# A joint input projection in exact fp32 passes, changed to split products with two block buffers

## The reference, cut to what matters

```
h_ctx = layernorm(ctx) * (1 + scale_c) + shift_c        # 256 context tokens, 1024 channels
h_x   = layernorm(x)   * (1 + scale)   + shift          # 256 tokens, 1024 channels
u     = concat(h_ctx, h_x)                              # 512 tokens
z, xbc, dt, rwkv, gq, gk, gv, gd, og = split(u @ w_in)  # w_in: 1024 x 3504, the joint projection
```

## Time and profile before

| what | value |
|---|---|
| median of three runs | 2103.74 us |
| the profiled execution, device time | 2110.86 us |
| its span, first to last instruction | 2109.1 us |
| mean granted TensorE clock | 0.939 of full speed |
| TensorE busy | 1927.0 us (91%) |
| joint projection, first to last matmul | 908.3 to 1143.3 us |

### The profile page before, as it was taken

How to read it: one execution, slowest core, us unless ns; L and a number is a source line. 1 busy time by engine, 2 the same in 40 slices (tenths; PEclk the granted TensorE clock), 3 DMA queues, 4 the chain that set the end, 5 groups by cost and what they waited for, 6 DMA issues and landing times.

```text
span 2109.1 us, 33698 instructions
## 1 busy us (share of the span) xinstructions
PE 1927.0 (91%) x14454; PEld 1399.7 (66%) x14454; DVE 1001.6 (47%) x1382; ACT 644.9 (31%) x1004; POOL 216.0 (10%) x218
## 2 busy tenths in 40 slices
PE   6878999899998899989999779989899999999992
PEld 5758999889997899855766658874344444444440
DVE  4664554555554677756545664663221121111116
ACT  4334333444443533330033531421111111111110
POOL 0000000000000000002100014401111111121213
PEclk9878999999997999999899679989999999999997
DMA  9313555544442777546511000066998998998886
GB/s 326 101 61 113 189 187 179 171 146 160 141 161 78 262 245 250 165 149 192 160 50 43 0 13 4 3 264 244 398 382 342 380 383 345 377 376 350 329 345 253
DMA packets 191893, 438.68 MB, mean 208 GB/s; under 512 B 24208, under 2 KB 145552, under 8 KB 162448
## 3 DMA queue, kind: packets, MB, share of 16 engines
q1 hardware_dynamic: 156336, 352.02, 45.4%
q0 software_dynamic: 23040, 43.05, 6.0%
q10 hardware_dynamic: 12384, 41.69, 5.1%
HBM read 501.68 MB, written 26.21 MB: 250 GB/s over the span
## 4 chain that ended last, share of the span: by engine, by line
PE 81%; DVE 9%; DMA 4%; ACT 3%; issue 2%; SPq 0%; POOL 0%; ACTq 0%; DVEq 0%; POOLq 0%
PE psum L344 30%; PE psum L3324 15%; PE psum L3345 7%; PE psum L1538 6%; PE psum L3295 4%; PE psum L1545 2%; DMA mem<-in_exp_w_dram 2%; PE psum L2555 2%; ACT w_hi L400 1%; DMA mem<-in_na_w_qkv_dram 1%; DVE mem L3445 1%; PE psum L2539 1%; DVE w_lo L405 1%; PE psum L3085 1%; PE psum L564 1%
## 5 line engine op out<-in xcount | busy, mean ns | idle before, releaser
L405 DVE TENSOR_TENSOR w_lo<-mem,w_hi 128x2048 fp32r<-128x2048 f32 x122 | 279.3, 2291 | 266.5 <-ACT w_hi L400 263.9
L344 PE MATMUL psum<-x_hi,w_hi 128*128 128x256 f32 x1216 | 353.5, 291 | 4.6 <-DVE x_lo L551 4.6
L3324 PE MATMUL psum<-mem 128*64 128x512 f32 x1536 | 341.4, 597 | 7.8 <-DMA mem<-in_exp_w_dram 7.8
L344 PE MATMUL psum<-x_hi,w_lo 128*128 128x256 f32 x1216 | 347.4, 286 | 0.0
L344 PE MATMUL psum<-x_lo,w_hi 128*128 128x256 f32 x1216 | 346.8, 285 | 0.0
L400 ACT ACTIVATE w_hi<-mem 128x2048 fp32r<-128x2048 f32 x122 | 233.8, 1918 | 202.4 <-PE psum L344 187.5
L3324 PEld LDWEIGHTS psum<-mem 128*64 128x64 f32 x1536 | 110.5, 138 | 230.8 <-issue 213.7
L344 PEld LDWEIGHTS psum<-x_hi,w_hi 128*128 128x128 f32 x1216 | 237.2, 195 | 11.3 <-DVE w_lo L405 4.9
L344 PEld LDWEIGHTS psum<-x_lo,w_hi 128*128 128x128 f32 x1216 | 240.9, 198 | 0.7
L344 PEld LDWEIGHTS psum<-x_hi,w_lo 128*128 128x128 f32 x1216 | 239.7, 197 | 0.0
L3345 PE MATMUL psum<-mem 128*64 128x512 f32 x768 | 175.4, 598 | 2.4 <-issue 1.8
(11 more groups left out here) (494 smaller groups left out, 2982.3 us busy)
## 6 DMA issues: line engine op xcount, KB each, us to landing
mem<-in_exp_w_dram SPq DMA_DIRECT2D x192, 1024.0 KB
mem<-in_dil_w_qkv_dram SPq DMA_DIRECT2D x36, 1024.0 KB, 5.3
mem<-in_ada_w_dram POOLq DMA_DIRECT2D x48, 512.0 KB, 4.7
y_rows<-mem ACTq DMA_DIRECT2D x48, 512.0 KB
mem<-in_ffn_w_gate_dram SPq DMA_DIRECT2D x22, 1024.0 KB, 5.7
mem<-in_ffn_w_up_dram SPq DMA_DIRECT2D x22, 1024.0 KB, 5.6
mem<-in_ffn_w_down_dram SPq DMA_DIRECT2D x22, 1024.0 KB, 4.8
mem<-in_w_in_dram SPq DMA_DIRECT2D x13, 1024.0 KB, 6.7
```

The source lines that it names most:

```text
L344: ins = pe.matmul(out, lhs[a], rhs[b], start=start and k == 0, stop=stop and k == 2, **kw)
L405: dve.tensor_tensor(w_lo[n % SLOTS][:, 0, :], ring[:, n % SLOTS, :], w_hi_f[n % HI][:, 0, :], ALU.subtract).then_inc(S("w_split"), 1)
L3324: ins = pe.matmul(psum[r, up, :].rearrange("p (a n) -> p a n", a=2), xg[:, b % 2, c, x * P + 64 * e:x * P + 64 * e + 64], w_up[s][e][:, :, ...
```

## The change

The projection is done in split products, and its buffers are arranged anew:

- The six ring slots get fixed roles. Slots 0 and 1 hold the raw and low parts of the activations (`u_raw`, `u_lo`), slots 2 and 3 the raw weight block of even and odd items (the low part is written over the raw one), slots 4 and 5 their high parts. So two blocks are in flight and not six: the load of block n (n of 2 or more) waits until block n-2 is used (`mix_in_sp`).
- Blocks 0 and 1 are cast and subtracted ahead of time (`mix_hi_act` in the first block's code on ScalarE, `mix_lo` on VectorE, block 1's behind the activations). For each later block the cast is put into ScalarE's list, and the subtraction into GpSimd's, at one half of a job of the block before: the first half of its second job, or the second half of its only job (`next_split`).
- The activations are split too: `ctx_hi_act`, `ctx_lo_dve`, `x_hi_act` (ScalarE, 8 chunks) and `x_lo_dve` (VectorE, two dependent operations for each of 8 chunks). TensorE's first job waits chunk by chunk.
- Block 0 is 128 columns wide in place of 32. The z blocks stand between xbc blocks and dt before the last xbc block. SyncE holds the loads of `w_out` until the projection is done.

```diff
-    mix_items = ([(GD0, 32, "chan"), (GQ0, 256, "chan"), (GV0, 256, "tok_all"), (OG0, 256, "tok_x")]
-                 + [(XBC0 + 256 * i, 256, "chan") for i in range(4)] + [(DT0, 16, "dt")]
-                 + [(Z0 + 256 * i, 256, "tok_x") for i in range(2)]
+    mix_items = ([(GD0, P, "chan"), (GQ0, 256, "chan"), (GV0, 256, "tok_all"), (OG0, 256, "tok_x"),
+                  (XBC0, 256, "chan"), (Z0, 256, "tok_x"), (XBC0 + 256, 256, "chan"), (Z0 + 256, 256, "tok_x"),
+                  (XBC0 + 512, 256, "chan"), (DT0, 16, "dt"), (XBC0 + 768, 256, "chan")]
                  + [(RW0 + 256 * i, 256, "chan") for i in range(4)] + [(RW0 + 1024, 128, "chan")])
...
     def mix_in_sp(sp):
-        for c0, w, _ in mix_items:
-            load(sp, cols(d["w_in_2"][0], c0, w), KC, w)
+        for m, (c0, w, _) in enumerate(mix_items):
+            n = MIX + m
+            sp.wait_ge(S("item_used"), n - SLOTS + 1 if m < 2 else n - 1)
+            sp.dma_start(slot(MIX_RAW[m % 2], KC, w), cols(d["w_in_2"][0], c0, w)).then_inc(S(f"slot_loaded{n % SLOTS}"), 16)
+            sp_items[0] += 1
+
+    def mix_hi_act(act, m):
+
+        n, w = MIX + m, KC * mix_items[m][1]
+        act.wait_ge(S(f"slot_loaded{n % SLOTS}"), 16 * (n // SLOTS + 1))
+        if m < 2:
+            act.wait_ge(S("item_used"), MIX - 3 + m)
+        act.activation(mix_hi[m % 2][:, 0, 0:w], ring[:, MIX_RAW[m % 2], 0:w], ACT.Copy).then_inc(S("w_hi"), 1)
+
+    def mix_lo(eng, m):
+
+        w = KC * mix_items[m][1]
+        eng.wait_ge(S("w_hi"), split_no(MIX + m))
+        eng.tensor_tensor(w_lo[MIX_RAW[m % 2]][:, 0, 0:w], ring[:, MIX_RAW[m % 2], 0:w], mix_hi_f[m % 2][:, 0, 0:w],
+                          ALU.subtract).then_inc(S("w_split"), 1)
...
+    def next_split(h):
+
+        m, part = divmod(h, 2)
+        n, k, parts = MIX_JOBS[m][:3]
+        return n + 1 if part == (0 if parts == 2 else 1) and k == parts - 1 and 2 <= n + 1 < len(mix_items) else None
...
-                ins = pe.matmul(psum[0:wd, b, 0:ALL], w[:, c, k * P:k * P + wd], uT[:, c, :], start=c == 0,
-                                stop=c == KC - 1)
+                if m == 0:
+                    if c == 0:
+                        pe.wait_ge(S("x_split"), X_NO["ctx"] + 2)
+                    x_part(pe, "x", c)
+                ins = split_product(pe, bank(b), [a[:, c, k * P:k * P + P] for a in w], [a[c // 4][:, c % 4, :] for a in u], c == 0,
+                                    c == KC - 1)
...
     def mixed_act(act):
-            if what == "move" and n % 2 == 0:
+            if what == "half" and next_split(n):
+                mix_hi_act(act, next_split(n))
+            elif what == "move" and n % 2 == 0:
...
     def mixed_pool(pool):
-            if what == "gla":
+            if what == "half" and next_split(n):
+                mix_lo(pool, next_split(n))
+            elif what == "gla":
...
     def block2_dve(dve):
         x_rows_dve(dve)
-        for c in range(1, KC, 2):
-            x_out(dve, c)
+        for h in range(2):
+            ctx_lo_dve(dve, h)
+        for c in range(KC):
+            x_lo_dve(dve, c)
+        mix_lo(dve, 1)
         mixed_dve(dve)
```

More of the change, by code:

```diff
@@ L132 @@
 SECOND_USE = {
+    "ctx_hi": ("na_bias_ready", 8),
     "sd_skip": ("sd_a", 1), "sd_xdt_n": ("sd_u", 1),
@@ L1288, in block1_act @@
         act.wait_ge(S("mod_in"), 16 * 8)
+        for m in range(2):
+            mix_hi_act(act, m)
         residual_act(act, MOD)
@@ L1319, in block1_dve @@
         mod_dve(dve)
+        mix_lo(dve, 0)
         residual_dve(dve)
@@ L1477, in program @@
     top[0] = stage_top
-    uT = alloc(KC, ALL)
+    u_hi_f, u_hi = zip(*(both(f"u_hi{h}", top[0] + 4 * h * ALL, 4, ALL) for h in range(2)))
+    u_lo = [both(f"u_lo{h}", ring_at + 4 * h * ALL, 4, ALL)[1] for h in range(2)]
+    u_raw = mem[:, ring_at:ring_at + KC * ALL].rearrange("p (c n) -> p c n", c=KC)
+    top[0] += KC * ALL
     ctx_tok = mem[:, mod_at + 6 * D:mod_at + 6 * D + NT * D].rearrange("p (t c) -> p t c", t=NT)
@@ L1511, in mix_jobs, with jobs_at @@
                         yield n, k, 2, xbcT[:, (c0 - XBC0) // P + k, :], 1.0
+    MIX_RAW, MIX_HI = (2, 3), (4, 5)
+    assert MIX % SLOTS == MIX_RAW[0] and W_OUT % SLOTS == 0
+    mix_hi_f, mix_hi = zip(*(both(f"mix_hi{q}", ring_at + q * SLOT, 1, SLOT) for q in MIX_HI))
     def mix_in_sp(sp):
-        for c0, w, _ in mix_items:
-            load(sp, cols(d["w_in_2"][0], c0, w), KC, w)
-    MIX_JOBS = list(mix_jobs())
-    J_OG, J_XBC, J_RW = 5, 6, 17
+        for m, (c0, w, _) in enumerate(mix_items):
[14 more added lines that the diff above has]
+                          ALU.subtract).then_inc(S("w_split"), 1)
+    MIX_JOBS = list(mix_jobs())
+    def jobs_at(lo, hi):
+        return [m for m, j in enumerate(MIX_JOBS) if lo <= mix_items[j[0]][0] < hi]
+    XBC_JOBS, RW_JOBS = jobs_at(XBC0, DT0), jobs_at(RW0, GQ0)
+    J_DT, J_RW, J_OG = jobs_at(DT0, RW0)[0], RW_JOBS[0], jobs_at(OG0, OG0 + 1)[0]
+    def next_split(h):
+        m, part = divmod(h, 2)
+        n, k, parts = MIX_JOBS[m][:3]
+        return n + 1 if part == (0 if parts == 2 else 1) and k == parts - 1 and 2 <= n + 1 < len(mix_items) else None
     def mix_moved(eng, m):
@@ L1544, in mix_half_pe @@
                 for c in range(KC):
-                    ins = pe.matmul(bank(b, width, a * width), uT[:, c, tiles[a] * P:(tiles[a] + 1) * P], w[:, c, :],
-                                    start=c == 0, stop=c == KC - 1)
+                    tok = slice(tiles[a] * P, (tiles[a] + 1) * P)
+                    ins = split_product(pe, bank(b, width, a * width), [v[c // 4][:, c % 4, tok] for v in u], [v[:, c, :] for v in w],
+                                        c == 0, c == KC - 1)
         if part == 1:
@@ L3475, in block2_act @@
         norm_n["act"] += 1
-        for c in range(0, KC, 2):
-            x_out(act, c)
+        for c in range(KC):
+            x_hi_act(act, c)
         mixed_act(act)
```

48 lines of the change are left out of this document (30 added, 18 removed).

## The result

The changed kernel takes 2145.35 us (median of 4 runs, 2135.7 to 2148.79) where the kernel before takes 2104.39 in the same comparison: 1.018 times as long by the ratio on record, 95% interval 1.015 to 1.021 (the two medians differ by 41 us, a factor of 1.019). The forecast was slower, 2130 us, 26 us above its own base; the direction is right, the size 15 us short. The profiled span is 2147.0 us, 37.9 longer than the one before.

A forecast was written before the change was run, and what follows sets the result against it. Projection bound by TensorE alone. Bookkeeping 255 against 233 us, +22, plus 1 for dt and 3 for the clock: +26, so 2137 us against the profiled 2110.86, 2130 us against the median; range 2104 to 2152 us.

The forecast's parts named there:

- TensorE's side: Projection matmuls: channel and token jobs save 28 and 6 us, dt costs 4 and 2 more; 28 us saved.
- When a block is ready: Blocks 1 to 15: cast and subtraction, 6.6 us with handovers, often come late; new kernel's stalls sum to 60 us.
- the hand sum: Block 12: ready at 1101.2, TensorE standing from 1091.3 after one 5.54 us job; a wait of 9.9 us.
- the bookkeeping: Projection: four queues carried forward entry by entry in list order; 255 us against 233 for the kernel before, +22.
- The waits that were there: Kernel before, projection: 6 us of stalls (1.4 + 5.0) taken off the new 60, leaving 54.
- The clock: Behind some five long stalls: up to 1.7 us each, 0 to 9 us together; 3 taken.
- Rival (c): Projection: clock stays low after stalls, 9 for 3, and late modulation rows add two per block for 8; 2152 us, chance 0.15.
- GpSimd against VectorE: Twelve full subtractions: each can hold a two-input VectorE operation for up to 4.52 us, the whole instruction.
- the sum with 41 us of stalls: Projection: VectorE gets through beside GpSimd's subtractions, as by a shared port; stalls 41 us, not 60.
- Rival (a): Projection: VectorE is not held by the long subtraction; 237 against 233 us in the bookkeeping, 2112 us, chance 0.17.
- Rival (b): Blocks 4 to 10: casts reached one half earlier, TensorE idle under 10 us; -18, 2086 us, chance 0.13.
- Nothing behind the projection: After the projection: nothing moves; `w_out` is loaded from 1143 on and used after 1331.

The follow-up runs named there:

- Experiments 6: Changed kernel with all subtractions on VectorE, block 12's split ahead of the modulation sum, and dt as a channel job: 2105.90 us, 1.0004 of the kernel before.
- experiment 9: The kernel before with only its dt job turned into a channel job, no split: 2098.97 us, 0.9980 of the kernel before.
- Experiment 3: Changed kernel with extra matmuls, results overwritten, while TensorE waits for blocks 2, 3, 4, 6, 8, 12 and 13: 2136.75 us, 1.0128 of the kernel before.
- Experiment 1: Changed kernel with every subtraction at its old place in the order but in VectorE's queue: 2120.63 us, 1.0066 of the kernel before.
- experiment 2: Changed kernel with GpSimd's subtraction of a full block cut into four pieces of 512 elements: 2141.18 us, 1.0152 of the kernel before.
- Experiment 4: Changed kernel with block 12's cast and subtraction ahead of the modulation sum and GLA's end: 2138.67 us, 1.0136 of the kernel before.

## Why the prediction was right, and where it fell short

**TensorE's side: right.** The balance has 30.2 us saved at full clock; the prediction had 28 with dt's slow stretch. dt's 96 loads took 10.34 + 5.9 = 16.2 us against 10.6 before: +5.6, where +4 and +2 were foreseen. A channel job took 5.54 us, as foreseen.

**When a block is ready: right in place, and up to GLA's end nearly in size.** Predicted and measured waits: block 1, 1.8 and 1.24; block 2, 7.2 and 6.83; block 3, 1.4 and 1.35; block 4, 6.9 and 7.09; the GLA multiply, 3.9 and 2.55; block 6, 2.7 and 3.47; block 8, 4.3 and 4.03; GLA's end, 5.5 and 3.37; block 12, 12.6 (9.9 by the hand sum) and 6.80; block 13, 5.1 and 1.14; block 14, 7.3 and 6.69. Up to GLA's end, 33.7 predicted (34.8 with the small ones) and 29.9 measured. Carrying the queues forward, entry by entry, works there. Of the signs that it named, GpSimd's subtraction has 31 us of TensorE's waits (expected some 50), VectorE the other 14, and the wait before block 12 is 6.80 us (10 to 13).

**Blocks 12 and 13: 10 us too much between them**, and this is where the two errors meet. The hand sum had block 12 ready 15.4 us behind the modulation sum, and it was 15.3 us (1111.64 to 1126.93). But TensorE reached the wait late: the job ahead of it ran at the low clock, 8.5 us from 1111.64 in place of 5.54, which makes 6.8 of the 9.9. This is no price of a wait: the modulation sum pulls the clock down, in the kernel before as well. The 2.7 us that the bookkeeping had on top did not show. Block 12's own two jobs took 13.4 us in place of 11.1, which covered 2.3 us of block 13's wait. I had waits of 60 us at full clock; the chip had 44.6, and part of the difference as slow matmuls.

**The waits that were there: 5 us too many.** The bookkeeping took 6 us of waits off for the kernel before, where the earlier trace rows has TensorE idle for 1.1 us. So the 15 us too much after and the 5 too much before leave the difference 10 too high.

**The clock: the step that failed.** I sized it from one row, at 1.7 us a stall, set it at 0 to 9 us and took 3, arguing that part of it only eats time that TensorE would stand anyway; dt added 1. The slow stretches sum to some 23 us above before, and 20 of them stand behind seven waits, so this term was some six times too small. A stall costs more than the 1.7 us of the earlier trace rows: the matmuls behind the four waits of 6.7 to 7.1 us took 3.0, 2.2, 2.3 and 3.0 us longer, and behind the three waits of 3.4 to 4.0 us, well below the 6.60 us of that row, 1.6, 3.1 and 4.9 us. And I took a third of my own upper bound. The clock does not fall behind stalls alone: it was 0.63 in the 21.0 us around dt, where TensorE was busy the whole time. Experiments 6 and 9 show that dt costs about 6 and 4 us of clock, its own second half with it. But most of that is in the kernel before too (6.6 us against 8.0), so it isn't what the forecast missed.

**The sum.** Predicted +26: waits +54, matmuls at full clock -31 (the bookkeeping), clock and dt +4, which makes 27 (26 by the rounding of 255 against 233). Measured +38.4: waits +43.7, matmuls -30.2, clock and rest +24.9. The waits were 10 us too high, the clock 21 too low. The two errors have opposite signs, so the sum is off by less than the clock is, and that the forecast came within 15 us is in part luck. "250 to 265 us" for the stretch was wrong: 273.4. Experiment 3 tempers it: of 10.4 us of slow clock that extra matmuls bought off, 6.1 stayed, since waits grow where it falls away. That much of my reason for a low term, that part of it only eats time that TensorE would stand anyway, holds. Rival (c), 2152 us, named that mechanism and is nearest to the measured time, but its second half did not happen: it put 16 us on late rows of the modulation product, and the waits before blocks 3 to 8 sum to 18.5 us, where the forecast had 19.2. A row does stand in the chain behind block 4's wait, as the forecast had it.

**GpSimd against VectorE: right.** L1892 took 4.81 us beside a subtraction of 4.50 us, where the only row before was 1.3 us long. The rule of the Trainium skill (SBUF, section Who interferes with whom), that the loser waits for the whole instruction, holds here for one more than three times as long; the sum with 41 us of stalls, in which VectorE gets through, is refuted for the instruction that was held from start to end. Experiment 1 takes the same subtractions off GpSimd and returns 24 us. Rival (a), no hold, is refuted by L1892; what the hold alone costs was not measured apart from the slower subtraction. What neither the rule nor I foresaw is experiment 2: pieces back to back hold VectorE as one long instruction, at least for L1896.

**Rival (b), faster: refuted at its own point.** It asked for less than 10 us of idling in blocks 4 to 10; it was 7.09 + 2.55 + 3.47 + 4.03 = 17.1 us, before GLA's end.

**Nothing behind the projection: right.** 37.9 us of span against 38.4 of projection.

**Open.** When VectorE gets in between two GpSimd instructions; how the 24 us of experiment 1 divide between the hold and the shorter subtraction; and whether a third buffer would let the split pay, which wasn't tried.

## What to carry to other kernels

A matmul saved by a preparation on another engine is worth what the preparation leaves of it: here 30.2 us of matmuls against 43.7 us of waits. Experiment 4 shows that a cast behind waiting entries of a queue makes such waits; that the depth of two does is argued, not tested. So carry all queues forward entry by entry before believing the gain. Then price every new gap of a busy TensorE with the slow job that follows it, from several rows behind stalls of this kernel, and look for stretches of narrow matmuls, which cost clock while fully busy (16 columns in dt, one in the modulation sum); they are worth an edit of their own, as experiment 9 shows. And do not give GpSimd a long operation on SBUF tensors beside a VectorE that is half full: VectorE did the same subtractions in half the time, and its own busy time fell.

## What the runs showed of the hardware that I had not expected

- VectorE was held by four GpSimd pieces back to back as by one instruction: 3.75 us for an operation of 0.43 us.
- TensorE, busy for 21.00 of 21.00 us with many matmuls of 16 columns, was granted 0.63 of its clock. With dt as a channel job the kernel before went from 0.96 to 0.99 over the projection.
- The clock also fell in the modulation sum, 32 matmuls of one column with TensorE busy throughout: 0.74 in 7.4 us of the kernel before, and 8.63 us for the job behind it in place of 7.08.
- Extra matmuls during waits raised the granted clock from 0.85 to 0.91 and, without the dt block's narrow ones, from 0.94 to 0.97.
- Taking 27.5 us of subtraction onto VectorE made its busy time 10.9 us shorter.
